# Position-bias tables in a two-block decoder: 128 stored copies per row, or one mirrored copy read in overlapping stretches

## The reference, cut to what matters

```python
def rel_bucket(dist):                      # 32 buckets of the distance t_query - t_key
    n = jnp.maximum(dist, 0)
    large = 16 + (jnp.log(jnp.maximum(n, 1) / 16) / math.log(128 / 16) * 16).astype(jnp.int32)
    return jnp.where(n < 16, n, jnp.minimum(large, 31))
...
bias_c = rel_bias[rel_bucket(dist_c)]      # compressed: dist_c = t - (16 c + 31)
s_c = einsum(q, kcc) + bias_c;  p_c = masked_softmax(s_c, dist_c >= 0)
...
s = einsum(q, k) + rel_bias[rel_bucket(dist)]   # selected and window: every key at or before t
p = masked_softmax(s, dist >= 0)
...
# second block, sliding window, with a sink per head
s = s + rel_bias_2[bucket(dist)];  s = where((0 <= dist) & (dist < 128), s, -inf)
m = maximum(max(s), sink);  p = exp(s - m) / (sum(exp(s - m)) + exp(sink - m))
```

## Time and profile before

| | us |
|---|---|
| median of 3 runs | 2372.04 (2371.59 to 2375.6) |
| the profiled execution | 2371.15 |
| its span, first to last instruction | 2369.4 |
| PE busy in the span | 2236.5 (94%) |
| DVE, ACT, POOL busy | 1450.2, 978.6, 153.7 |
| mean granted clock | 0.972 |

### The profile page before, as it was taken

The page is one execution under the profiler, slowest core; times in us unless marked ns, Lnnn a source line. Parts: engine busy times, 40 slices in busy tenths (PEclk is TensorE's granted clock), DMA queues, the critical chain, the costliest instruction groups (busy, mean ns, idle before and its releaser), DMA issues.

```text
span 2369.4 us, 42194 instructions
## 1 busy us (share of the span) xinstructions
PE 2236.5 (94%) x18002; PEld 2207.5 (93%) x18002; DVE 1450.2 (61%) x1773; ACT 978.6 (41%) x1311; POOL 153.7 (6%) x105
## 2 busy tenths in 40 slices
PE   7499779989999999999999899999999999999997
PEld 7498778989999999999999789998999999999997
DVE  6344556568767767677778666656554445544554
ACT  4123245434444343344333356634443344334443
POOL 5000000020000000000025200030000000000010
PEclk9799989999999999999999899999999999999999
DMA  6878763348878788788777432454555555555552
GB/s 223 163 243 303 186 157 129 136 150 321 298 262 309 267 298 316 253 297 305 285 283 239 153 115 75 162 167 150 171 196 187 188 179 177 196 182 188 182 178 89
DMA packets 222234, 495.28 MB, mean 209 GB/s; under 512 B 12296, under 2 KB 30523, under 8 KB 209761
## 3 DMA queue, kind: packets, MB, share of 16 engines
q1 hardware_dynamic: 214368, 481.06, 58.7%
q0 software_dynamic: 7504, 11.45, 3.6%
q10 hardware_dynamic: 176, 0.07, 0.0%
HBM read 484.12 MB, written 8.39 MB: 208 GB/s over the span
## 4 chain that ended last, share of the span: by engine, by line
PE 85%; DMA 6%; DVE 4%; POOL 2%; ACT 2%; issue 1%; ACTq 0%; DVEq 0%; POOLq 0%; SPq 0%
PE bank L816 78%; DMA m_RAW<-in_nsa_w_in 3%; PE bank L883 2%; DMA m_RAW<-in_cmp_w_k 1%; PE bank L846 1%; PE bank L952 1%; ACT m_WHI L1192 1%; DVE m_WLO L1514 1%; DMA m_RAW<-in_w_mod 1%; POOL m_SQ L1841 1%; POOL m_SQ L1842 1%; PE bank L855 1%; POOL m_SR L1846 0%; PE bank L991 0%; ACT m_SP L1272 0%
## 5 line engine op out<-in xcount | busy, mean ns | idle before, releaser
L1514 DVE TENSOR_TENSOR m_WLO<-m_RAW,m_WHI 128x1024 fp32r<-128x1024 f32 (+2 forms) x712 | 874.5, 1240 | 761.0 <-ACT m_WHI L1192 739.4
L1192 ACT ACTIVATE m_WHI<-m_RAW 128x1024 fp32r<-128x1024 f32 (+2 forms) x712 | 738.4, 1045 | 1094.2 <-PE bank L816 935.7
L816 PE MATMUL bank<-m_HI,m_WHI 128*128 128x256 f32 x2816 | 822.5, 292 | 45.3 <-DVE m_WLO L1514 26.8
L816 PE MATMUL bank<-m_LO,m_WHI 128*128 128x256 f32 x2816 | 806.4, 286 | 0.0
L816 PE MATMUL bank<-m_HI,m_WLO 128*128 128x256 f32 x2816 | 805.7, 286 | 0.0
L816 PEld LDWEIGHTS bank<-m_HI,m_WHI 128*128 128x128 f32 x2816 | 550.4, 195 | 49.7 <-issue 30.2
L816 PEld LDWEIGHTS bank<-m_LO,m_WHI 128*128 128x128 f32 x2816 | 550.3, 195 | 1.4
L816 PEld LDWEIGHTS bank<-m_HI,m_WLO 128*128 128x128 f32 x2816 | 549.7, 195 | 0.0
L816 PE MATMUL bank<-m_H3H,m_WHI 128*128 128x256 f32 x1408 | 397.0, 282 | 0.0
L816 PE MATMUL bank<-m_H3L,m_WHI 128*128 128x256 f32 x1408 | 395.6, 281 | 0.0
L816 PE MATMUL bank<-m_H3H,m_WLO 128*128 128x256 f32 x1408 | 395.5, 281 | 0.0
(11 more groups left out here) (286 smaller groups left out, 1703.9 us busy)
## 6 DMA issues: line engine op xcount, KB each, us to landing
m_RAW<-in_w_ff SPq DMA_DIRECT2D x128, 1024.0 KB, 5.2
m_RAW<-in_w_mod SPq DMA_DIRECT2D x96, 1024.0 KB, 5.8
m_RAW<-in_ffn_w_in SPq DMA_DIRECT2D x88, 1024.0 KB, 6.6
m_RAW<-in_ffn_w_out SPq DMA_DIRECT2D x44, 1024.0 KB, 5.8
m_RAW<-in_nsa_w_in SPq DMA_DIRECT2D x40, 1024.0 KB, 8.1
m_RAW<-in_nsa_w_out SPq DMA_DIRECT2D x16, 1024.0 KB, 5.1
m_RAW<-in_w_out SPq DMA_DIRECT2D x16, 1024.0 KB, 5.1
m_RAW<-in_w_in SPq DMA_DIRECT2D x10, 1024.0 KB, 5.3
```

The lines of the kernel that those rows point to most:

```text
L816: mm = e.matmul(o, lhs, rhs, start=start and i == 0, stop=fin and i == 2, skip_group_check=True)
L1192: e.activation(WHI[u % 4][:, 0:(z - a) * ncol], raw[:, a * ncol:z * ncol], ACT.Copy).then_inc(a_hi, 1)
L1514: e.tensor_tensor(WLO[u % 4][:, 0:m], raw[:, a * ncol:z * ncol], WHI[u % 4][:, 0:m].bitcast(F32), ALU.subtract).then_inc(v_lo, 1)
```

## The change

The one-hot constant is built for rising distances (entry i of a row is distance i - 128), the table in HBM holds each row once (16 x 384), and one `table_out` DMA per table writes it. Partition p now reads the 256 numbers that begin at 1 + p, so neighbouring partitions read stretches that overlap in all but one number, and `biasA[p, head, x]` is the bias of distance p + x - 127. Key j therefore stands at x = 255 - j, and the readers on DVE go from right to left (`from_right`, a step of -1, in `cscore` -16). `every` gets one entry for each table instead of four. Waits for the table are for 16 instead of 64.

```diff
-    down = np.clip(255 - np.arange(384), -127, 255)
-    oh = np.concatenate([onehot(down, 256), onehot(down, 128)], axis=1)
+    up = np.clip(np.arange(384) - 128, -127, 255)
+    oh = np.concatenate([onehot(up, 256), onehot(up, 128)], axis=1)
...
     every.extend([None] * 4)
-    every.extend(lambda i=i: put("table_out", 0, i, st["cursor"]) for i in range(4))
+    every.append(lambda: put("table_out", 0, st["cursor"]))
     every.append(lambda: put("makez", 0))
...
     every.extend([None] * 6)
-    every.extend(lambda i=i: put("table_out", 1, i, st["cursor"]) for i in range(4))
+    every.append(lambda: put("table_out", 1, st["cursor"]))
...
-    toep = [nc.dram_tensor(n, [16, 128, 384], F32, kind="Internal").ap() for n in ("toepA", "toepB")]
+    toep = [nc.dram_tensor(n, [16, 384], F32, kind="Internal").ap() for n in ("toepA", "toepB")]
...
+    def from_right(a, first, n, jump=1):
+        return bass.AP(tensor=a.tensor, offset=a.offset + first, ap=[list(d) for d in a.ap[:-1]] + [[-jump, n]])
...
-                cv = [biasA[:, 4 * g:4 * g + 4, o:256:16] for o in (159, 31)]
+                cv = [from_right(biasA[:, 4 * g:4 * g + 4, :], 255 - o, n, 16) for o, n in ((159, 7), (31, 15))]
...
-                    bias = biasA[:, i, :] if i < 16 else biasB[:, 2 * (i - 16) + br, :] if i < 24 else causal[:, :]
+                    if i < 24:
+                        table = biasA[:, i, :] if i < 16 else biasB[:, 2 * (i - 16) + br, :]
+                        bias = from_right(table, 255, 256) if blk else from_right(table, 127, 128)
+                    else:
+                        bias = causal[:, :] if blk else causal[:, 128:256]
                     ins = e.tensor_tensor_reduce(
-                        out=sp[:, o:o + n], in0=src, in1=bias if blk else bias[:, 128:256],
+                        out=sp[:, o:o + n], in0=src, in1=bias,
...
-            return bass.AP(tensor=t.tensor, offset=t.offset + 127 + h0 * 128 * 384, ap=[[383, 128], [128 * 384, n], [1, 256]])
+            return bass.AP(tensor=t.tensor, offset=t.offset + 1 + h0 * 384, ap=[[1, 128], [384, n], [1, 256]])
...
-                rows = bass.AP(tensor=src.tensor, offset=src.offset, ap=[list(src.ap[0]), [0, 128], [1, 384]])
-                e.dma_start(toep[t][4 * i:4 * i + 4], rows).then_inc(l_table[t], 16)
+                e.dma_start(toep[t], (R16a, R16b)[t][:, :]).then_inc(l_table[t], 16)
...
-                w.wait_ge(l_table[0], 64)
+                w.wait_ge(l_table[0], 16)
```

More of the change, by code:

```diff
@@ L1805, in from_table @@
         def from_table(t, h0, n):
-            return bass.AP(tensor=t.tensor, offset=t.offset + 127 + h0 * 128 * 384, ap=[[383, 128], [128 * 384, n], [1, 256]])
+            return bass.AP(tensor=t.tensor, offset=t.offset + 1 + h0 * 384, ap=[[1, 128], [384, n], [1, 256]])
         for name, *arg in ORDER:
             if name == "table_out":
-                t, i, c = arg
-                src = (R16a, R16b)[t][4 * i:4 * i + 4, :]
+                t, c = arg
                 w.wait_ge(b_out[5], filled(("toep",), 5))
@@ L1851, in gpsimd_program @@
                 e.dma_start(sinT[:, :], A["c_sin"]).then_inc(l_rope, 16)
-                w.wait_ge(l_table[1], 64)
+                w.wait_ge(l_table[1], 16)
                 e.dma_start(biasB[:, :, :], from_table(toep[1], 0, 16)).then_inc(l_biasB, 16)
```

## The result

| | before | after |
|---|---|---|
| median (range, runs) | 2373.25 (2371.59 to 2375.6, 4) | 2310.31 (2307.25 to 2314.27, 4) |
| the profiled execution | 2371.15 | 2311.51 |
| its span | 2369.4 | 2309.7 |
| mean granted clock | 0.972 | 0.983 |

The ratio is 0.9735 with a 95% interval of [0.9717, 0.9753]: 62.9 us faster. 2310 was predicted, with a range of 2299 to 2328.

The account below looks back on a forecast made before the run. PE was taken as the bound, so only its stalls or lower clock could give time back. 2371.15 - 38.2 (table A) - 24.2 (table B) + 1.0 (L952 chunks) = 2309.8 us, predicted as 2310, range 2299 to 2328.

Parts of the forecast that it names:

- Table A's write, -38.2: PE stall in 80.73 to 134.02 us: writing table A once gives back 38.2 us, bounds about 31 to 39.
- Table B's write, -24.2: PE stall within 271 to 340 us: writing table B once gives back 24.2 us, bounds 18 to 27.
- The L952 chunks earlier, +1.0: L952 chunks come three weight chunks earlier: 1 us charged for the first load, bounds 0 and 16.
- Reads 0: Overlapping reads of `biasA` and `biasB`: no change taken; upper bound 175 engine-us per MB, 16 us for each table.
- slow reads: Rival at the bias reads: overlapping reads are slow like the writes, 2310 + 24 = 2334 us; chance 0.10.
- Right to left 0: DVE operands with a negative step: no cost taken; upper bound a doubling, 35.7 us of DVE.
- The sum: Whole kernel: 2371.15 - 38.2 - 24.2 + 1.0 = 2309.8 us, predicted as 2310.
- The signs: Profile after: no PE wait over 3 us in 60 to 300 us, clock 1.00 from some 50, later stages 61 us earlier.
- Writes innocent, only their bytes count: Rival at the table writes: 6.3 MB at 45 engine-us per MB return only 18 us, 2353 us; chance 0.03.
- Hot 24 KB: Rival at the table reads: engines queue at one small piece of HBM, slower than before, 2383 us; chance 0.03.
- starving ring: Rival at the earlier L952 chunks: weight loads fall behind at 2.4 MB per 9.3 us, 2318 us; chance 0.10.
- first rival: The slow reads rival at the bias reads, 2334 us, chance 0.10; it called the slow DMA the one whose source repeats.

Follow-up runs that it names:

- order_kept: Against after: three empty entries behind each table write, so L952 chunks, Z, table reads and table B's write stand where before had them; 2309.33 us.
- tableA_128: Against after: table A written as 128 copies again by four DMAs, each partition reading its own copy; 2351.35 us.
- tableB_128_late: Against after: table B written as 128 copies by four DMAs, with three empty entries behind table A's write so they stand as in before; 2334.8 us.
- rows_apart: Against after: the 16 rows of table A lie 48 KB apart in HBM instead of 1.5 KB, still written once; 2315.31 us.
- spread_write: Against after: 3 MB of unread writes added where table A's writes stood, four DMAs of 768 KB from all 128 partitions; 2311.6 us.
- spread_repeat: Against after: 3 MB of unread writes added, from all 128 partitions, each partition's same piece four times (step 0); 2310.25 us.
- narrow_distinct: Against after: 3 MB of unread writes added, four DMAs each from 4 partitions (0 to 15 in all), 128 different pieces of each; 2349.32 us.

## Why the prediction was right, point by point

- **Table A's write, -38.2.** Right. The first reader starts 39.5 us earlier, 37.1 in order_kept, and putting the copies back costs 41.0. The upper bound of 39 was too tight for two of these three. A part of the difference is the clock, and not the tables: in the first 60 us, ahead of them, it is 0.94 in after and 0.91 in order_kept and before, which is 1 to 2 us; and in tableA_128 it is 0.96 in 200 to 282.6 us, where before had 1.00.
- **Table B's write, -24.2.** Right: 64.1 - 39.5 = 24.6 by the readers' start times, and 24.5 by tableB_128_late. The count of a half-clock stretch (time low, less time idle) fits this sum; it wasn't measured apart.
- **The L952 chunks earlier, +1.0.** Not measurable: order_kept is 1.0 faster, within its spread. PE's waits there in after are 0.7 us. (The rival's 2.4 MB in 9.3 us are 258 GB/s, not 270; after moves 277 and 250 GB/s in its two windows, and PE doesn't starve.)
- **Reads 0.** Right for this layout (49 engine-us per MB), and by more luck than the text admits. The reason given, that a read of HBM is like the row at 50 and not like a write, is no reason: rows_apart is a read of HBM with the same overlaps at 122. The upper bound of 175 was sound, and a chance of 0.10 for slow reads rested on no row.
- **Right to left 0.** Right: 2 to 3 ns each, 96 times, are 0.2 us at most.
- **The sum.** 2309.8 against 2311.51 for the profiled execution, and 2310 against 2310.31 for the median. That the last agree to 0.3 us is luck: runs of after spread over 7 us. In the traces A and B gave 64.1 us against 62.4 predicted, and 4.6 of it are gone again at the first reader of `biasB`. In that stretch one wait of PE grew; in 1150 to 1300 us of after it is

```profile
PE bank L900 <- POOL m_SR L1852: 15.5, 3, 6.2
```

  and at the same work of before, in 1210 to 1310 us:

```profile
PE bank L896 <- POOL m_SR L1846: 12.5, 3, 5.2
```

  That is 3.0 us. But order_kept has 12.6 us there and the stretch between the last reader of `biasA` and the first of `biasB` is no shorter than in after (932.3 us against 930.6; before 926.0). Over all kernels of this case the stretch takes 926.0 to 932.4 us and the wait 12.5 to 15.8, with the table writes in the old places or in the new; the one trace of before is the shortest. So this looks like the spread of executions, and a small cost of the new timing isn't excluded.
- **The signs.** After 60 us PE waits for nothing over 1.4 us up to 300 us, weight loads land in 5.3 us in 50 to 120 us, the clock is 1.00 in 50 to 300 us, and the later stages come 59.5 us earlier where 61 was said.
- **Rivals.** "Writes innocent, only their bytes count" (2353) is refuted by spread_write: 3 MB more are free. "Hot 24 KB" (2383) and the starving ring (2318) did not come. The slow reads exist, in another layout.
- **What made a write slow** was left open: the prediction priced it by its row (175 per MB) without a cause. Under its first rival it even named the repetition as what was special; spread_repeat shows that this is harmless and narrow_distinct that the few neighbouring partitions do it.

## What to carry to other kernels

Price a DMA in engine time per MB from its own row, not in bytes: 3 MB cost nothing here from 128 partitions and 39 us from 16 neighbours, since they took 89.8% of the time of all 16 engines (in 84 to 96 us) that the weight loads also needed. Look at which partitions a DMA touches; 16 of them four apart were as good as 128. What such a DMA costs depends on what stands beside it (24.5 or 33.4 us for the same four), so try a transfer that has to be slow at more than one place.

## What was not expected of the hardware

- 768 KB from 4 partitions, four such DMAs on their way together, landed in 36.2 us (0 to 15), 13.8 us (four apart) and 55.8 us (0 to 7 with 32 to 39) in the median, with equal packets.
- A source step of 0 costs nothing: 7.5 against 7.4 us.
- Overlapping reads of 2.10 MB by 128 partitions took 49 engine-us per MB from rows 1.5 KB apart and 122 from rows 48 KB apart; without overlap, from rows 192 KB apart, 50.
- An fp32 operand of DVE with a step of -1 took 354 ns against 352 with +1, and 349 to 354 over the kernels of this case.
